# Where the transposes of x stand between two sublayers, and how y is squared and scaled

## The chip, the cores and the metric

One NeuronCore of a Trainium2 chip runs the whole kernel in one launch. The metric is device time in microseconds of that launch, the median of several executions. Engines are named as the profile names them: PE (TensorE), DVE (VectorE), ACT (ScalarE), POOL (GpSimd), SP (SyncE, which here only starts DMAs).

## The reference

Four decoder layers over a sequence of 256 tokens of width 1024, in float32. Each layer is a half-step SwiGLU FFN, a token mixer, and a second FFN. The mixers are a short gated convolution, a dilated windowed attention, an mLSTM, and the convolution again.

```python
def rmsnorm(x, g):
    y = x * rsqrt(mean(x * x, axis=-1) + 1e-6)
    return y * g

def swiglu(x, wg, wu, wd):
    return (silu(x @ wg) * (x @ wu)) @ wd       # 1024 -> 2816 -> 1024

for i in range(4):
    x = x + 0.5 * rmsnorm(swiglu(rmsnorm(x, g[0]), ...), g[1])
    x = x + rmsnorm(mixer_i(rmsnorm(x, g[2])), g[3])
    x = x + 0.5 * rmsnorm(swiglu(rmsnorm(x, g[4]), ...), g[5])
```

So between two of the twelve sublayers there is always the same seam, called a joint here: norm of y over all 1024 columns, update of x, norm of x over all 1024 columns.

## The kernel before, in words

**Tiling.** The 256 tokens are two tiles of 128 (tile 0 and tile 1), one token to a partition. Weights come in pieces of 128x2048 floats (1 MB), 352 of them, in a fixed order; SP loads them into three raw buffers. For accuracy each product is made of three: ACT rounds a piece to `w_high` (`high`, line 1039), DVE subtracts to get `w_low` (`low`, line 1421), and the other operand is split in the same way, so that `products` (lines 487 to 489) issues high x high, high x low and low x high. Split pieces stand in a ring of six. A raw buffer is free for the next load once `low` has read it, a ring slot once TensorE has used the piece (`piece_used`).

**Order of the work.** Every engine has its own program, a list written out by hand that it works off in order; a wait on a semaphore holds all that stands behind it in that engine's list. There is no planner.

**A joint.** The products of a sublayer end with y in four PSUM banks: tile 0 in two halves of 512 columns, tile 1 in two. `y_ready` tells of tile 0 as a whole, `piece_used` of tile 1 as a whole. For each tile ACT squares both halves with a running sum (`square_y`, line 1048), POOL adds the two sums and epsilon (`of_y`, line 1839) and raises to the power -1/2 (line 1843), DVE multiplies both halves by the gain (line 1432) and then updates x (line 1436). ACT squares x (line 1057), POOL adds epsilon (line 1830) and takes the power (line 1833), and DVE writes the normed xn (`pre_norm`, line 1443). TensorE turns xn in eight transposes into two banks (`transpose_x`, line 522), ACT copies them as the high half of xT (line 1063) and DVE subtracts the low half (line 1449). Only then can the next sublayer's products (`arriving`, lines 500, 503 and 506) start, which take half of the columns at a time as they arrive.

**Which transposes stand where.** Tile 0's stand at the head of each sublayer, behind all products of the one ahead. Tile 1's stand in an FFN inside its second block; in a mixer they stand at the head of tile 1's first three units (`first_three`). In the FFN's last part TensorE takes tile 0 with the last three chunks, then tile 1 with the same three; within a chunk first half 0, then half 1.

**Beside it.** At a joint ACT also makes `high(w0 + 3)` (after a mixer `high(w0 + 2)` too), where w0 is the first piece of the next sublayer, and DVE the `low` of the same. In `joint_part` of DVE, `low(w0 + 3)` stands between the update of tile 1 and its `pre_norm`; in that of ACT, `high(w0 + 3)` stands right behind the square of x of tile 0. In the attention, the 256 tokens are also wanted sorted by class (position modulo 4): `into_classes` copies the high half of xT on ACT in four copies (line 1228) and the low half on DVE in two (line 1630), all after tile 1's transposes; `rotate` is the rotary embedding on DVE, `copy_out` moves a unit's projection out of PSUM (line 1222), and `transpose_qk` (line 761) waits until some of the first six banks are free. Unit 6 is the first that reads the sorted x.

Of the kernel before, what the change touches and what calls it, by code (L numbers as in the profile page):

```python
# [25 lines left out]
ALU = mybir.AluOpType  # L26
ACT = mybir.ActivationFunctionType

P = 128
# [96 lines left out]
def build(nc, x_in, gains, stream, gate_w, gate_b, conv_k, ident_in, rope_in, att_mask_in, ml_mask_in,  # L126
          tri_in, out):
    with ExitStack() as ctx:
# [19 lines left out]
        mean_x = sb("mean_x", [P, TILES])  # L148
        mean_eps = sb("mean_eps", [P, 2 * TILES])
# [14 lines left out]
        def x_arrived(which):  # L164

            if KINDS[sub_now[0]] == "att":
                return xT_first[which]
            return xT_view(which)

# [58 lines left out]
        eps_added = sem("eps_added")  # L228
# [166 lines left out]

        def xT_bank(joint, t, b):
# [21 lines left out]
        def att_bank(quarter, n):  # L418
            if quarter == 0 and n < 6:
                return FIRST_BANKS[n // 3][n % 3]  # L420
            return 4 + n % 2

# [27 lines left out]
        def _(sp):  # L450
# [29 lines left out]
            sp.wait_ge(stored, 16 * TILES)  # L480
# [3 lines left out]
        def _(pe):  # L484
# [27 lines left out]
            def transpose_x(joint, t):  # L512
# [3 lines left out]
                for b in range(2):  # L516
# [6 lines left out]
                    last.then_inc(xT_in_psum, 1)  # L523

# [4 lines left out]
            def ffn(sub):  # L529
# [52 lines left out]
                def down(c, p, t, turn=0):  # L582

                    weights_ready(p + RING * turn)
                    for half in range(2):
                        for j in range(FT):
                            cols = slice(j * D + half * 512, j * D + half * 512 + 512)
                            tok, at = slice(t * P, (t + 1) * P), h_slot(FT * c + j)
                            if t == 1 and half == 1 and j == FT - 1 and c < CHUNKS - 1:

                                for part in range(2):
# [7 lines left out]
                                            c == 0 and j == 0, c == CHUNKS - 1 and j == FT - 1)  # L599
                    if t == 1:  # L600
                        last.then_inc(piece_used, 1)
                    elif c == CHUNKS - 1:
                        last.then_inc(y_ready, 1)
# [16 lines left out]
                transpose_x(sub, 0)  # L620
# [18 lines left out]
                for t in range(TILES):  # L639
                    for c in range(CHUNKS - 3, CHUNKS):  # L640
                        if t == 0:
                            pe.wait_ge(hT_split, s0 + splits_up_to(FT * c + 1))
                        down(c, w0 + down_piece(c), t)

            def project_out(sub):

                p0 = w_of(sub + 1) - OUT_PIECES
                for t in range(TILES):
                    tok = slice(t * P, (t + 1) * P)
                    for q in range(OUT_PIECES):  # L650
# [5 lines left out]
                        for k4 in range(4):  # L656
                            k, cols = 4 * (q // 2) + k4, slice(k4 * 512, (k4 + 1) * 512)
# [4 lines left out]
                    if t == 0:  # L662
                        last.then_inc(y_ready, 1)
# [11 lines left out]
            def tokens_first(slot, acc, t, xh=None, xl=None):  # L675

                xh, xl = (x_arrived(0), x_arrived(1)) if xh is None else (xh, xl)
                for k in range(KD):
                    tok, cols = slice(t * P, (t + 1) * P), slice(k * 256, (k + 1) * 256)
                    last = products(acc, xh[:, k, tok], xl[:, k, tok], w_high[:, slot, cols],  # L680
                                    w_low[:, slot, cols], k == 0, k == KD - 1)
                return last
# [43 lines left out]
            def attention(sub):  # L726
                w0 = w_of(sub)

                def unit(quarter, n):
# [4 lines left out]
                    if quarter == 0 and n == 6:  # L734

                        pe.wait_ge(x_by_class, KD // 2)
                        pe.wait_ge(x_low_by_class, 2)
# [4 lines left out]
                def transpose_qk(quarter, r):  # L742

                    pe.wait_ge(rope_done, 2 * QK * quarter + r + 1)
                    if r < 2 and quarter == 0:

                        pe.wait_ge(proj_copied, 3 + r)
                    elif r == 1 and quarter:

                        pe.wait_ge(oT_split, ot_before(sub) + 2 * quarter - 1)  # L750
                    elif r == 10:

                        pe.wait_ge(qkT_done, 2 * QK * quarter + 1)
                        if quarter:
                            pe.wait_ge(oT_split, ot_before(sub) + 2 * quarter)
# [4 lines left out]
                    for j in range(2):  # L760
                        last = nc.tensor.transpose(ps[:, QKT_BANK[r], j * P:(j + 1) * P],  # L761
# [133 lines left out]
                for q in (2, 3):  # L895
                    last = project_out_of(0, q, (7,))
                last.then_inc(y_ready, 1)
                for q in range(OUT_PIECES):
                    project_out_of(1, q, tuple(range(4 * (q // 2), 4 * (q // 2) + 4))).then_inc(piece_used, 1)

# [127 lines left out]
        def _(act):  # L1028
# [12 lines left out]
            def square_y(joint, t):  # L1041
                if t == 0:
                    act.wait_ge(y_ready, joint)
                else:
                    act.wait_ge(piece_used, BASE[joint])

                for half in range(2):
                    nc.scalar.activation(xn[:, t, half * 512:(half + 1) * 512], ps[:, Y_BANK + 2 * t + half, :], ACT.Square,  # L1048
# [905 lines left out]
```

## Time and profile before

| | us |
|---|---|
| median of 3 runs (2075.20 to 2076.81) | 2075.58 |
| the profiled execution's own time | 2076.98 |
| its span, first to last instruction | 2075.2 |
| PE busy | 2042.1 (98%) |
| DVE busy | 1170.3 (56%) |
| ACT busy | 970.0 (47%) |
| POOL busy | 53.3 (3%) |

Busy time is the union of an engine's instructions; for PE the ends are modelled, so short stalls between two products may not show as idle. Times given as positions count from the start of the span. "[0.97 <-ACT xT_both L1063]" behind a row means that the engine was idle for 0.97 us before it and that this instruction ended the wait.

### The profile page before, as it was taken

The page shows a single profiled execution, that of the slowest core. Times are in us where ns is not written, and L with a number is a line of the kernel's source. Part 1 is how long each engine was busy: PE and PEld are TensorE (multiplying, and loading weights), DVE is VectorE, ACT ScalarE, POOL GpSimd, SP SyncE. Part 2 cuts the span into 40 slices and gives each one's busy share as a digit, 9 for nine tenths or more (in the row PEclk, how much of TensorE's full clock was granted, in tenths as well). Part 3 has the DMA queues.
Part 4 walks back from the last instruction along what each step waited for, and adds up shares of the span by engine and source line. Part 5 has one row for each costly group of instructions (what it writes and reads, how often), then busy time and mean ns, then how long its engine had stood idle before and what let it go on. Part 6 is the DMA issues. An engine that isn't in the chain of part 4 may idle for free.

```text
span 2075.2 us, 36087 instructions
## 1 busy us (share of the span) xinstructions
PE 2042.1 (98%) x14956; PEld 1899.5 (92%) x14956; DVE 1170.3 (56%) x1328; ACT 970.0 (47%) x1184; POOL 53.3 (3%) x100
## 2 busy tenths in 40 slices
PE   7999999999999999999999999999999999999998
PEld 6999989998999899988998999898999899998997
DVE  6555765556555656556555645565545655676453
ACT  5444444444444656655444534544434444444442
POOL 0000000000000000001000000000000000000000
PEclk9999999999999999999999999999999999999999
DMA  8544646455554543435554654544554655555541
GB/s 315 201 185 161 231 154 244 182 184 203 201 186 166 180 160 143 163 122 203 199 186 170 225 204 181 194 162 152 202 203 174 223 183 184 192 192 193 203 182 62
DMA packets 55983, 386.41 MB, mean 186 GB/s; under 512 B 6592, under 2 KB 6976, under 8 KB 10816
## 3 DMA queue, kind: packets, MB, share of 16 engines
q1 hardware_dynamic: 52416, 372.66, 48.9%
q10 hardware_dynamic: 3456, 12.13, 1.7%
q8 instruction: 88, 1.44, 0.3%
q14 instruction: 23, 0.19, 0.0%
HBM read 383.71 MB, written 1.05 MB: 185 GB/s over the span
## 4 chain that ended last, share of the span: by engine, by line
PE 96%; ACT 2%; DVE 1%; issue 1%; DMA 0%; POOL 0%; ACTq 0%; POOLq 0%; SPq 0%; DVEq 0%
PE ps L487 29%; PE ps L489 29%; PE ps L488 29%; PE ps L500 2%; PE ps L503 2%; PE ps L506 2%; PE ps L522 1%; ACT w_high L1039 1%; PE ps L807 1%; PE ps L761 0%; ACT xT_both L1063 0%; PE ps L783 0%; PE ps L817 0%; PE ps L577 0%; ACT xn L1048 0%
## 5 line engine op out<-in xcount | busy, mean ns | idle before, releaser
L1421 DVE TENSOR_TENSOR w_low<-raw,w_high 128x2048 fp32r<-128x2048 f32 x352 | 804.4, 2290 | 316.2 <-ACT w_high L1039 315.8
L487 PE MATMUL ps<-xT_both,w_high 128*128 128x256 f32 x2656 | 737.1, 278 | 0.0
L488 PE MATMUL ps<-xT_both,w_high 128*128 128x256 f32 x2656 | 735.6, 277 | 0.0
L489 PE MATMUL ps<-xT_both,w_low 128*128 128x256 f32 x2656 | 735.4, 277 | 0.0
L1039 ACT ACTIVATE w_high<-raw 128x2048 fp32r<-128x2048 f32 x352 | 670.5, 1911 | 41.7 <-DMA raw<-stream 25.3
L488 PEld LDWEIGHTS ps<-xT_both,w_high 128*128 128x128 f32 x2656 | 499.9, 188 | 0.0
L487 PEld LDWEIGHTS ps<-xT_both,w_high 128*128 128x128 f32 x2656 | 499.4, 188 | 0.1
L489 PEld LDWEIGHTS ps<-xT_both,w_low 128*128 128x128 f32 x2656 | 498.6, 188 | 0.0
L1073 ACT ACTIVATE region<-ps 128x256 f32<-128x256 f32 x176 | 67.6, 384 | 659.4 <-PE ps L489 642.2
L487 PE MATMUL ps<-w_high,oT_hi 128*128 128x512 f32 (+1 forms) x944 | 348.6, 369 | 1.5 <-DVE oT_lo L1662 1.5
L488 PE MATMUL ps<-w_low,oT_hi 128*128 128x512 f32 (+1 forms) x944 | 347.5, 368 | 0.0
L489 PE MATMUL ps<-w_high,oT_lo 128*128 128x512 f32 (+1 forms) x944 | 347.4, 368 | 0.0
L1457 DVE TENSOR_TENSOR region<-region,ps 128x256 f32<-128x256 f32 x176 | 74.0, 420 | 343.5 <-ACT region L1073 343.3
L487 PE MATMUL ps<-w_high,xT_both 128*128 128x256 f32 (+1 forms) x832 | 254.2, 305 | 3.6 <-DVE xT_both L1630 1.9
L489 PE MATMUL ps<-w_high,xT_both 128*128 128x256 f32 (+1 forms) x832 | 246.8, 297 | 0.0
L488 PE MATMUL ps<-w_low,xT_both 128*128 128x256 f32 (+1 forms) x832 | 246.3, 296 | 0.0
L487 PEld LDWEIGHTS ps<-w_high,oT_hi 128*128 128x128 f32 x944 | 177.8, 188 | 31.3 <-issue 1.9
L489 PEld LDWEIGHTS ps<-w_high,oT_lo 128*128 128x128 f32 x944 | 177.7, 188 | 29.9
L488 PEld LDWEIGHTS ps<-w_low,oT_hi 128*128 128x128 f32 x944 | 177.8, 188 | 29.0
L487 PEld LDWEIGHTS ps<-w_high,xT_both 128*128 128x128 f32 x832 | 157.3, 189 | 11.2 <-issue 4.4
L489 PEld LDWEIGHTS ps<-w_high,xT_both 128*128 128x128 f32 x832 | 157.3, 189 | 5.5
L488 PEld LDWEIGHTS ps<-w_low,xT_both 128*128 128x128 f32 x832 | 157.5, 189 | 4.8
(163 smaller groups left out, 1141.7 us busy)
## 6 DMA issues: line engine op xcount, KB each, us to landing
raw<-stream SPq DMA_DIRECT2D x352, 1024.0 KB, 4.8
gain<-gains ACTq DMA_DIRECT2D x23, 512.0 KB, 4.7
x<-x_in SPq DMA_DIRECT2D x2, 512.0 KB, 6.1
out<-x SPq DMA_DIRECT2D x2, 512.0 KB, 2.7
gain<-gains SPq DMA_DIRECT2D x1, 512.0 KB, 5.3
att_mask<-att_mask_in SPq DMA_DIRECT2D x1, 384.0 KB, 5.3
region<-rope_in SPq DMA_DIRECT2D x1, 256.0 KB, 4.9
ml_mask<-ml_mask_in SPq DMA_DIRECT2D x1, 128.0 KB, 5.1
```

The costliest lines, as they stand in the source:

```text
L487: nc.tensor.matmul(acc, lh, rh, start=start, stop=False)
L488: nc.tensor.matmul(acc, lh, rl, start=False, stop=False)
L489: return nc.tensor.matmul(acc, ll, rh, start=False, stop=stop)
L500: nc.tensor.matmul(acc, x_arrived(0)[:, k, tok], w_high[:, slot, cols], start=k == 0, stop=False)
L503: nc.tensor.matmul(acc, x_arrived(1)[:, k, tok], w_high[:, slot, cols], start=False, stop=False)
L506: last = nc.tensor.matmul(acc, x_arrived(0)[:, k, tok], w_low[:, slot, cols], start=False, stop=k == KD - 1)
L522: last = nc.tensor.transpose(ps[:, xT_bank(joint, t, b), k * P:(k + 1) * P], xn[:, t, f:f + P], ident[:, :])
L807: last = nc.tensor.transpose(ps[:, bank, n * P:(n + 1) * P], probs[:, 2 * pair + e, t, col * P:(col + 1) * P], ident[:, :])
L1039: nc.scalar.activation(w_high[:, p % RING, :], raw[:, p % RAW, :], ACT.Copy).then_inc(piece_high, 1)
L1073: nc.scalar.activation(silu[:, i % 2, :], ps[:, GU_BANK + i % 2, 0:SEQ], ACT.Silu).then_inc(silu_done, 1)
L1421: nc.vector.tensor_tensor(w_low[:, p % RING, :], raw[:, p % RAW, :], w_high[:, p % RING, :], ALU.subtract).then_inc(piece_split, 1)
L1457: nc.vector.tensor_tensor(h[:, i % 2, :], silu[:, i % 2, :], ps[:, GU_BANK + i % 2, SEQ:2 * SEQ], ALU.mult).then_inc(h_ready, 1)
```

## The change

TensorE: the transposes of tile 0's xn for the next sublayer are issued ahead of the last six products of the sublayer before (in an FFN, ahead of the last chunk's second half of tile 1; in a mixer, ahead of the last two k of the last output piece). In a mixer tile 1's transposes go inside tile 0's third unit, behind k = 3. In an FFN's last part TensorE now takes half 0 of a tile for all three chunks and then half 1, and each half of y is announced by itself. ACT squares y by halves, DVE multiplies by the gain by halves; for tile 1 the copy of tile 0's xT stands between the two halves. The additions of epsilon go from POOL to DVE; POOL keeps the power. `high` and `low` of piece w0 + 3 move behind other work. In the attention the sorting copies go by tile instead of by columns (2 on each engine), tile 0's stands ahead of tile 1's xT, the copies out of units 0 and 1 and their rotations too, and the first quarter's q and k transposes use banks 2 and 3. At the very end x of tile 1 is updated and written in two halves, the second from ACT's DMA queue.

```diff
@@ sync
-                sp.dma_start(out[t * P:(t + 1) * P, :], x[:, t, :]).then_inc(stored, 16)
+                cols = slice(0, 512 if t else D)
+                sp.dma_start(out[t * P:(t + 1) * P, cols], x[:, t, cols]).then_inc(stored, 16)
@@ tensor
+            def transpose_next(sub):
+                if sub + 1 < SUBLAYERS:
+                    transpose_x(sub + 1, 0)
...
-                            if t == 1 and half == 1 and j == FT - 1 and c < CHUNKS - 1:
+                            if t == 1 and half == 1 and j == FT - 1:
...
-                transpose_x(sub, 0)
+                if sub == 0:
+                    transpose_x(sub, 0)
...
                 for t in range(TILES):
-                    for c in range(CHUNKS - 3, CHUNKS):
-                        if t == 0:
-                            pe.wait_ge(hT_split, s0 + splits_up_to(FT * c + 1))
-                        down(c, w0 + down_piece(c), t)
+                    for half in range(2):
+                        for c in range(CHUNKS - 3, CHUNKS):
+                            p = w0 + down_piece(c)
+                            if t == 0 and half == 0:
+                                pe.wait_ge(hT_split, s0 + splits_up_to(FT * c + 1))
+                                weights_ready(p)
+                            if t == 1 and half == 1 and c == CHUNKS - 1:
+                                transpose_next(sub)
+                            for j in range(FT):
+                                cols = slice(j * D + half * 512, j * D + half * 512 + 512)
+                                tok, at = slice(t * P, (t + 1) * P), h_slot(FT * c + j)
+                                last = products(ps[:, Y_BANK + 2 * t + half, :], oT_hi[:, at, tok], oT_lo[:, at, tok],
+                                                w_high[:, p % RING, cols], w_low[:, p % RING, cols], False,
+                                                c == CHUNKS - 1 and j == FT - 1)
+                            if t == 1 and half == 1:
+                                last.then_inc(piece_used, 1)
+                            elif c == CHUNKS - 1:
+                                last.then_inc(y_ready, 1)
... project_out (and the same at the end of attention)
                         for k4 in range(4):
+                            if t == 1 and q == OUT_PIECES - 1 and k4 == 2:
+                                transpose_next(sub)
... first_three
-                if first == 0:
-                    transpose_x(sub, t)
-                        done = tokens_first(p % RING, acc, t)
+                        done = tokens_first(p % RING, acc, t, meanwhile=(lambda: transpose_x(sub, 1))
+                                            if t == 0 and i == 2 else None)
... attention
-                    if r < 2 and quarter == 0:
-                        pe.wait_ge(proj_copied, 3 + r)
+                    if quarter == 0:
+                        if r >= 2:
+                            pe.wait_ge(qkT_done, r - 1)
@@ scalar, joint_part
-                    high(w0 + 3)
+                    square_y(joint, 1, 0)
+                    xT(joint, 0)
+                    square_y(joint, 1, 1)
                     if before_ffn(joint):
-                        xT(joint, 0)
-                        square_y(joint, 1)
+                        high(w0 + 3)
+                        square_x(joint, 1)
                     else:
-                        square_y(joint, 1)
-                        xT(joint, 0)
-                    square_x(joint, 1)
+                        square_x(joint, 1)
+                        if KINDS[joint] == "att":
+                            att_copy_out(joint, 0, 0)
+                            into_classes(joint, 0)
+                            att_copy_out(joint, 0, 1)
+                        high(w0 + 3)
@@ vector
+            def gain_y(joint, t, half):
+                n, cols = TILES * (joint - 1) + t, slice(half * 512, (half + 1) * 512)
+                dve.wait_ge(y_mean, 2 * n + half + 1)
+                if half == 0:
+                    nc.vector.tensor_scalar(mean_first[:, t:t + 1], mean_y[:, t, 0:1], EPS / Y_SCALE[KINDS[joint - 1]] ** 2, None,
+                                            ALU.add).then_inc(y_eps, 1)
+                else:
+                    dve.wait_ge(y_eps, n + 1)
+                    nc.vector.tensor_tensor(mean_eps[:, t:t + 1], mean_y[:, t, 1:2], mean_first[:, t:t + 1],
+                                            ALU.add).then_inc(y_sum, 1)
+                dve.wait_ge(gain_landed, 16 * min(1 + 2 * joint, 2 * SUBLAYERS))
+                nc.vector.tensor_tensor(xn[:, t, cols], ps[:, Y_BANK + 2 * t + half, :], gain[:, 0, cols],
+                                        ALU.mult).then_inc(y_gained, 1)
...
             def pre_norm(joint, t):
+                dve.wait_ge(x_mean, TILES * joint + t + 1)
+                nc.vector.tensor_scalar(mean_eps[:, TILES + t:TILES + t + 1], mean_x[:, t:t + 1], EPS, None, ALU.add).then_inc(x_sum, 1)
                 dve.wait_ge(x_rstd, TILES * joint + t + 1)
... joint_part
                 if joint:
+                    gain_y(joint, 0, 0)
+                    gain_y(joint, 0, 1)
                     update_x(joint, 0)
...
-                if joint:
+                if joint:
+                    gain_y(joint, 1, 0)
+                    if joint < SUBLAYERS:
                         xT(joint, 0)
+                    gain_y(joint, 1, 1)
                     update_x(joint, 1)
...
-                else:
+                elif before_ffn(joint):
                     low(w0 + 3)
                     pre_norm(joint, 1)
+                else:
+                    pre_norm(joint, 1)
+                    if KINDS[joint] == "att":
+                        dve.wait_ge(loaded, CONSTS)
+                        rotate(joint, 0, 0)
+                        into_classes(joint, 0)
+                        rotate(joint, 0, 1)
+                    else:
+                        low(w0 + 3)
                 if before_ffn(joint):
                     times_up(joint, 0)
                 xT(joint, 1)
+                if KINDS[joint] == "att":
+                    low(w0 + 3)
@@ gpsimd
-                nc.gpsimd.tensor_scalar(mean_eps[:, n:n + 1], mean, EPS, None, ALU.add).then_inc(eps_added, 1)
+                        pool.wait_ge(x_sum, TILES * joint + t + 1)
```

## Rows read from the trace of the kernel before

**Rows 1.** List of TensorE's waits: line, tile, releaser, us in total, times, longest.
```profile
PE ps L500 <- ACT xT_both L1063: 5.4, 13, 1.0
PE ps L761 <- ACT region L1222: 3.0, 1, 3.0
PE ps L487 <- DVE xT_both L1630: 1.9, 1, 1.9
...
PE ps L979 <- ACT region L1338: 0.8, 1, 0.8
```

**Rows 2.** Timeline of TensorE, FFN to mixer: start, duration, operation, count, idle before.
```profile
198.06 1.03 PE L522 MATMUL ps<-ident,xn 128*128 128x128 f32 x8
200.06 0.74 PE L500 MATMUL ps<-w_high,xT_both 128*128 128x256 f32 x4 [0.97 <-ACT xT_both L1063]
200.79 0.74 PE L503 MATMUL ps<-w_high,xT_both 128*128 128x256 f32 x4
201.36 0.63 PE L506 MATMUL ps<-w_low,xT_both 128*128 128x256 f32 x4
201.83 0.63 PE L500 MATMUL ps<-w_high,xT_both 128*128 128x256 f32 x4
...
208.90 1.03 PE L522 MATMUL ps<-ident,xn 128*128 128x128 f32 x8
210.19 0.74 PE L500 MATMUL ps<-w_high,xT_both 128*128 128x256 f32 x4 [0.25 <-ACT xT_both L1063]
```

**Rows 3.** Chain that ended last: transposes inside an FFN block (start, us, what).
```profile
1432.90 0.87 PE ps L522 x8
```

**Rows 4.** Timelines of VectorE and TensorE, mLSTM to FFN.
```profile
1419.50 1.29 DVE L1443 SCALAR_TENSOR_TENSOR xn<-x,rstd_x,gain 128x1024 f32<-128x1024 f32 x1 [0.77 <-POOL rstd_x L1833]
...
1422.17 0.39 PE L489 MATMUL ps<-w_high,oT_lo 128*128 128x512 f32 x1
1422.40 1.03 PE L522 MATMUL ps<-ident,xn 128*128 128x128 f32 x8
1423.69 1.21 PE L500 MATMUL ps<-w_high,xT_both 128*128 128x512 f32 x4 [0.25 <-ACT xT_both L1063]
1424.73 0.62 PE L503 MATMUL ps<-w_high,xT_both 128*128 128x512 f32 x2
```

**Rows 5.** Windows in attention: us, busy by engine (instructions), granted clock, DMA.
```profile
688.00:690.00 2.00, 2.00 (x11) 2.00 (x11) 1.97 (x1) 0.00 (x0) 0.00 (x0) 0.50 0.90 373
690.00:692.00 2.00, 2.00 (x15) 2.00 (x14) 0.00 (x0) 0.11 (x1) 0.00 (x0) 0.74 0.36 61
```

**Rows 6.** Groups by line over the whole span: busy, mean ns, idle before.
```profile
L1039 ACT ACTIVATE w_high<-raw 128x2048 fp32r<-128x2048 f32 x352 | 670.5, 1911 | 41.7 <-DMA raw<-stream 25.3 <-PE ps L489 14.9 <-issue 1.2
...
L1833 POOL TENSOR_TENSOR rstd_x<-mean_eps,minus_half 128x1 f32<-128x1 f32 x24 | 13.6, 568 | 2.0
...
L1228 ACT ACTIVATE xT_both<-oT_hi 128x512 fp32r<-128x512 f32 x4 | 4.6, 1145 | 0.0
...
L1646 DVE TENSOR_SCALAR region<-region 128x2 f32<-128x2 f32 x16 | 2.7, 170 | 0.6
```

**Rows 7.** Timelines of ScalarE, VectorE and GpSimd around the first FFN's end.
```profile
189.97 0.60 ACT L1048 ACTIVATE xn<-ps 128x512 f32<-128x512 f32 x1 [3.27 <-PE ps L489]
...
195.85 1.28 DVE L1443 SCALAR_TENSOR_TENSOR xn<-x,rstd_x,gain 128x1024 f32<-128x1024 f32 x1 [2.18 <-POOL rstd_x L1833]
...
205.12 1.01 POOL L1830 TENSOR_SCALAR mean_eps<-mean_x 128x1 f32<-128x1 f32 x1 [4.55 <-ACT xn L1057]
```

**Rows 8.** Timelines of TensorE and VectorE at the kernel's end.
```profile
2067.97 0.39 PE L489 MATMUL ps<-w_high,oT_lo 128*128 128x512 f32 x1
...
2070.81 1.28 DVE L1436 SCALAR_TENSOR_TENSOR x<-xn,rstd_y,x 128x1024 f32<-128x1024 f32 x1 [0.34 <-POOL rstd_y L1843]
```

**Rows 9.** Timelines of VectorE and TensorE at the kernel's start.
```profile
17.43 1.28 DVE L1443 SCALAR_TENSOR_TENSOR xn<-x,rstd_x,gain 128x1024 f32<-128x1024 f32 x1
...
20.97 0.50 PE L487 MATMUL ps<-w_high,xT_both 128*128 128x512 f32 x1 [1.73 <-DVE w_low L1421]
```

More of the change, by code:

```diff
@@ L394, in before_ffn, with y_before @@
             return joint < SUBLAYERS and KINDS[joint] == "ffn"
+        def y_before(joint):
+            return sum(3 if kind == "ffn" else 2 for kind in KINDS[:joint - 1])
         def xT_bank(joint, t, b):
@@ L1086, in h_high, with att_copy_out, into_classes @@
                 nc.scalar.activation(oT_hi[:, h_slot(i), :], h[:, i % 2, :], ACT.Copy).then_inc(hT_high_done, 1)
+            def att_copy_out(sub, quarter, n):
+                i, t = att_unit(quarter, n)
+                if t == 0:
+                    act.wait_ge(proj_ready, att_piece(quarter, i) + 1)
+                else:
+                    act.wait_ge(piece_used, w_of(sub) + att_piece(quarter, i) + 1)
+                at = ps[:, att_bank(quarter, n), 0:256]
+                if i > QK:
+                    for half in range(2):
+                        row = (half if i == QK + 1 else 1 - half) * CW
+                        last = nc.scalar.activation(v_rest[row:row + CW, 2 * t + half, :],
+                                                    at[half * CW:(half + 1) * CW, :], ACT.Copy)
+                    last.then_inc(proj_copied, 1)
+                    return
+                to = qk[(i - 1) % 3][:, t, :] if i else v_first[quarter % 2][:, t, :]
+                nc.scalar.activation(to, at, ACT.Copy).then_inc(proj_copied, 1)
+            def into_classes(sub, t):
+                act.wait_ge(xT_high_done, 4 * sub + 2 * t + 2)
+                nc.scalar.activation(by_class(xT_high())[:, :, :, t * CT:(t + 1) * CT],
+                                     xT_first[0][:, :, t * P:(t + 1) * P].rearrange("p k (j r) -> p k r j", r=CLASSES),
+                                     ACT.Copy).then_inc(x_by_class, 1)
             def joint_part(joint):
@@ L1424, in update_x @@
             def update_x(joint, t):
                 n = TILES * (joint - 1) + t
-                dve.wait_ge(gain_landed, 16 * min(1 + 2 * joint, 2 * SUBLAYERS))
-                for half in range(2):
-                    cols = slice(half * 512, (half + 1) * 512)
-                    dve.wait_ge(y_mean, 2 * n + half + 1)
-                    nc.vector.tensor_tensor(xn[:, t, cols], ps[:, Y_BANK + 2 * t + half, :], gain[:, 0, cols],
-                                            ALU.mult).then_inc(y_gained, 1)
@@ L1434, in update_x @@
                 dve.wait_ge(y_gained, 2 * n + 2)
                 dve.wait_ge(y_rstd, n + 1)
-                nc.vector.scalar_tensor_tensor(out=x[:, t, :], in0=xn[:, t, :], scalar=rstd_y[:, t:t + 1], in1=x[:, t, :],
-                                               op0=ALU.mult, op1=ALU.add).then_inc(x_updated, 1)
+                for half in range(2 if joint == SUBLAYERS and t else 1):
+                    cols = slice(512 * half, 512 * (half + 1)) if joint == SUBLAYERS and t else slice(0, D)
+                    nc.vector.scalar_tensor_tensor(out=x[:, t, cols], in0=xn[:, t, cols], scalar=rstd_y[:, t:t + 1],
+                                                   in1=x[:, t, cols], op0=ALU.mult, op1=ALU.add).then_inc(x_updated, 1)
```

175 lines of the change are left out of this document (77 added, 98 removed).

## The prediction

> **What bounds the kernel now.** I read the page's busy shares, then the list of what TensorE waited for, then the timeline of each seam between sublayers ("joint"). TensorE is busy nearly all the span, so time can only come from its idle stretches, from products that run slowly, and from the two ends. The list of waits [rows 1] puts these idle stretches in few places: 13 waits for the copy of the transposed x (xT, line 1063), one before a transpose of q and k in attention, one for the reordered x (line 1630), one in the mLSTM sublayer. The timeline of a joint [rows 2] shows more than the list, because ends of products are modelled. I therefore measure from start to start. Eight transposes take 0.87 us [rows 3].
>
> *FFN to mixer* (198, 660, 1311 and 1790 us; four joints). Transposes start at 198.06, so the next product could start at 198.93; it starts at 200.06, a gap of 1.13. Four products then take 0.73, 0.57 and only then 0.47 us: 0.36 more. The ACT engine squares y of tile 1 before it copies tile 0's transposes, and DVE's low half of xT is late after that. The same stands at tile 1's transposes: 208.90 + 0.87 to 210.19 is a gap of 0.42, and the slow products come again (0.36). One such joint loses 1.13 + 0.36 + 0.42 + 0.36 = 2.27 us.
>
> *To an FFN* (293, 477, 944, 1128, 1423, 1607 and 1885 us; seven joints). Transposes at 1422.40 end at 1423.27, the next product starts at 1423.69: 0.42. Four 512-column products take 1.04 against 4 x 0.23 = 0.92: 0.12. One loses 0.53 [rows 4]; tile 1's transposes already stand inside a block here.
>
> *Attention only* [rows 1, 5]. The wait before the first q and k transpose is 3.0 us in the list and the one for the reordered x 1.9. A list entry is short by what the modelled end hides (0.97 where I measured 1.13 in [rows 2]), so I take 3.2 and 2.1. Then the granted clock falls: 0.50 in 688 to 690 and 0.74 in 690 to 692, that is the lower level of 1.2 GHz for some of it. Lost there: 2 x 0.50 + 2 x 0.26 = 1.5 us. It came after two long waits close together; the gaps of 1.13 alone brought no such fall. Sum 3.2 + 2.1 + 1.5 = 6.8 us. The chain behind it is ACT's: it makes xT of tile 1, a w_high and four reordering copies of 1.15 us each [rows 6] before TensorE gets what it waits for.
>
> **The change part by part.** The sum is against the profiled execution's own 2076.98 us (span 2075.2), which is 1.4 above the median of 2075.58.
>
> *Tile 0's transposes, moved ahead of the last six products.* TensorE's work is the same, in another order. The cover is six products of 0.23 us, 1.37 us: the first transposes are seen by ACT some 0.7 us after they start, so both halves of xT (0.60 each, overlapping) are there when the last product ends. It needs xn of tile 0 earlier by 1.37, at 196.69 instead of 198.06. Before, y's squaring started at 189.97 and xn was written at 195.85 + 1.28 = 197.13 [rows 7]. The new y path takes away one square (0.60) and one of two gain products (0.68) from the chain, since y's first half is done 4 us earlier, and changes POOL's addition for a DVE one. I work out: mean 190.7, DVE's small sum 0.17 (nearest row: a 128x2 one of 170 ns [rows 6]), POOL's power 0.57 [rows 6], update 191.6 to 192.9, square 194.1, sum 194.3, power 195.0, xn 196.3. So the wait is gone with 0.4 us to spare. After a mixer, DVE makes w_low of piece w0+2 between the update and the norm, and this piece can't come sooner (ACT waits for a free slot). xn comes at 1419.50 + 1.28 = 1420.78 as before; the transposes want it at 1422.40 - 1.37 = 1421.03 [rows 4]. Cover 0.25 us, thin. If it is gone, each of these joints loses what is missing.
>
> *Tile 1's transposes inside the third unit of tile 0 (mixers).* They want xn of tile 1 60 products of 0.1175 = 7.05 us after the first arriving product, at 206.0 in this joint. The last product now ends 0.87 later than before, which moves the y chain: mean 199.85, update ends 202.0, square 203.2, xn 205.5. w_low of piece w0+3 was ahead of this norm and now is behind it; TensorE needs that piece only 10 us on, so I cost it at nothing. Cover of the transposes: 12 products, 1.41 us, enough for the two copies.
>
> So both gaps of the four joints go, 4 x 2.27 = 9.1, and 7 x 0.53 = 3.7 at the joints to an FFN. Bounds: where the thin covers fail, 6 and 2; all of it at most.
>
> *Attention.* ACT's copies of units 0 and 1 and the reordering of tile 0 now stand ahead of xT of tile 1, and the q and k transposes no longer wait for a bank. A reordering copy has 1024 elements instead of 512; ACT has two instead of four. I take 2.1 us (two of 1.15 less one fixed part). In ACT's queue from the square of tile 1 (4.2 us after the first arriving product): copy 0.3, reorder 2.1, copy 0.3, w_high 1.85, xT 1.1, two w_high 3.7, copy 0.3, reorder 2.1, two small copies 0.65, w_high 1.85, copy 0.3, gives 4.2 + 14.5 = 18.7, with hops 19.2. TensorE's own work to unit 6 is 144 products x 0.1175 + 0.87 + 3 x 0.22 = 18.5. xT of tile 1 is some 0.3 late, unit 6 some 0.5 late. Of 6.8 us I leave 0.8 as waits, and expect no fall of the clock: gain 6.0. Bounds: 3 (one long wait and the fall stay) and 6.8.
>
> *mLSTM.* TensorE waits 0.8 at the gate rows for ACT, which waits for a piece's DMA [rows 1]. That chain starts from xT of tile 1, which gains a little more than TensorE does; I take 0.4 (0 to 0.8).
>
> *Last products in another order.* Two chunks of each FFN no longer split a 512-column product in two. Two of 256 columns take 2 x 0.1175 [rows 2], one of 512 takes 0.23 [rows 4]: 48 x 0.01 = 0.5 (0 to 0.6).
>
> *End of the kernel.* From the last product's start to the update's end it is 2070.81 + 1.28 - 2067.97 = 4.12 [rows 8]. One square (0.60 in [rows 7]) goes, and 0.2 is my estimate for the shorter addition and its hop; the update comes in two halves and the last write is of half the bytes from ACT's queue. 0.8 for the chain, 0.3 for the write: 1.1 (0.6 to 1.6).
>
> *Start of the kernel: a loss.* The epsilon for x of tile 1 was added on POOL while DVE was busy; xn was written at 17.43 right behind a w_low and the product at 20.97 waits for what DVE does next [rows 9]. Now the addition stands in DVE's queue behind that w_low, and POOL's power (0.57) and two hops come after it: 0.17 + 0.57 + 0.1 = 0.8 later. Tile 0 wins some 0.15. Net -0.6 (-0.9 to +0.2).
>
> A POOL addition of 128x1 elements took 1.01 us at 205.12 while DVE was busy with a w_low; the power, a longer operation, takes 0.57 [rows 6, 7]. The Trainium skill (SBUF — State Buffer, section "SBUF: two separate sides") says that POOL and a DVE operation with two SBUF inputs lock one port pair against each other for a whole instruction. The trace agrees. By that rule alone the addition, taken off POOL, would give back most of that 1.01 us in each chain of tile 1. The queue's order says no: the DVE addition stands behind the same w_low before an FFN, and before a mixer that w_low has been moved. I take nothing for it.
>
> Sum: 9.1 + 3.7 + 6.0 + 0.4 + 0.5 + 1.1 - 0.6 = 20.2. Own time after 2056.8; median 2055.4.
>
> **The rivals.**
> *A, the waits move into the last products.* xn of tile 0 comes 0.3 to 0.8 us too late (small DVE operations and hops cost more than I took; covers are 0.4 and 0.25). 11 joints x 0.5 = 5.5 less gain: about 2061. Against it: each duration of the chain has a row.
> *B, attention stays bound by ACT and DVE.* The strided copy of 1024 elements costs more, or a w_high in between waits for its DMA; a long wait and the half clock stay: 3 to 4 less gain, 2059. For it: my margin there is already negative.
> *C, slower than before.* TensorE's queue is in order, so a late xn now holds six products and all behind them. If xn came later than TensorE by more than 20.2 / 11 = 1.84 us beyond what I have, the sum turns. With 2.5 us a joint, and the clock at half after it (1.5 a time as in attention), 11 x 4.0 = 44 against 20: about 2079 to 2100. Against it: xn was written 0.9 us before the old transposes.
> *D, no change.* The gap after the transposes is TensorE's own (weights against identity) and not ACT's copy. Then 9.1 and 3.7 mostly stay, and attention and the end give 7: 2068; if attention stays too, 2074. Against it: inside an FFN block eight transposes take 0.87 us in all in the chain that ended last, with no stall behind them [rows 3].
>
> **How the numbers follow.** Forecast 0.62, A 0.17, B 0.12, C 0.03, D 0.03, more gain than I see 0.03. The likeliest gives 2055.4; the range reaches from 2052.8 (all upper bounds) to 2061.0 (A). About 0.2% (4.2 us) is what a measurement can tell from no change: faster 0.94, same 0.03, slower 0.03.
>
> **What would show it.** Right: no gap over 0.3 us at transposes of a joint; products at 0.47 per four right after them; the wait before the first q and k transpose gone and the clock at full through attention; the power of tile 1 at the start behind w_low and the first product behind it near 21.6 instead of 20.97; from the last product to the last update 3.3 us. Wrong: TensorE waits for xn (line 1443's operation) in its list of waits, or the clock falls in a joint.

## The result: slower, 2098.4 us

The changed kernel takes 2098.38 us (median of 4 runs, 2097.22 to 2098.88) against 2075.53 for the kernel before in the same comparison: a ratio of 1.0108 [1.0091, 1.0126], 23 us slower. The prediction said 2055.4, with a range up to 2061.0. The profiled execution has a span of 2097.1 us.

The list of what TensorE waited for (line, tile, releaser, us in total, times, longest), of the changed kernel, answers to [rows 1]:
```profile
PE ps L538 <- DVE xn L1504: 8.0, 1, 8.0
PE ps L503 <- DVE w_low L1470: 2.5, 1, 2.5
PE ps L516 <- ACT w_high L1078: 1.7, 1, 1.7
PE ps L503 <- DVE oT_lo L1737: 1.5, 1, 1.5
PE ps L503 <- ACT xn L1144: 1.2, 1, 1.2
PE ps L1009 <- DVE region L1862: 0.5, 1, 0.5
```
The 13 waits for the copy of xT (5.4 us) and the one before the q and k transposes (3.0) are gone. Of the one for the reordered x (1.9) there is left a wait of 1.2 at the same place in attention, ahead of unit 6 (the line with L1144); the prediction left 0.8 in attention. The first three lines are the start of the kernel. The list adds up to 15.4 us, that of the kernel before to 26.0, and yet the kernel is slower.

The timelines of TensorE at the first joint from an FFN to a mixer, changed kernel, answering to [rows 2]: tile 0's transposes inside the last products, then tile 1's inside a unit.
```profile
202.74 1.04 PE L538 MATMUL ps<-ident,xn 128*128 128x128 f32 x8
203.53 0.48 PE L503 MATMUL ps<-w_high,oT_hi 128*128 128x512 f32 x1
...
205.00 0.63 PE L516 MATMUL ps<-w_high,xT_both 128*128 128x256 f32 x4
205.47 0.63 PE L519 MATMUL ps<-w_high,xT_both 128*128 128x256 f32 x4
...
212.00 1.03 PE L538 MATMUL ps<-ident,xn 128*128 128x128 f32 x8
212.79 0.37 PE L503 MATMUL ps<-w_high,xT_both 128*128 128x256 f32 x1
```
The first product of the mixer starts when its turn comes (205.00), and the groups of four take 0.47 at once instead of 0.74 and 0.57. Tile 1's eight transposes take 0.79 and nothing waits behind them.

So the loss is in no wait. The page of the profile shows it in the largest groups: line, engine, operation, count, busy us, mean ns of one. The products with xT moving and weights stationary (6912 of 7968 stand in FFN blocks; three lines of 2656, one shown of before and two of the changed kernel) took 278 and 277 ns before and take 282 and 281 now:
```profile
L487 PE MATMUL ps<-xT_both,w_high 128*128 128x256 f32 x2656 | 737.1, 278 | 0.0
```
```profile
L503 PE MATMUL ps<-xT_both,w_high 128*128 128x256 f32 x2656 | 747.7, 282 | 0.0
...
L505 PE MATMUL ps<-xT_both,w_low 128*128 128x256 f32 x2656 | 746.0, 281 | 0.0
```
These durations overlap, so I read the distance from start to start. Two whole FFN blocks (96 products of 256 columns, xT moving, weights stationary) with nothing between them: the first product and the 512-column one behind the last, before:
```profile
61.50 0.29 PE L487 MATMUL ps<-xT_both,w_high 128*128 128x256 f32 x1
...
72.40 0.39 PE L487 MATMUL ps<-w_high,oT_hi 128*128 128x512 f32 x1
```
and in the changed kernel:
```profile
64.01 0.28 PE L503 MATMUL ps<-xT_both,w_high 128*128 128x256 f32 x1
...
75.37 0.40 PE L503 MATMUL ps<-w_high,oT_hi 128*128 128x512 f32 x1
```
72.40 - 61.50 = 10.90 us against 75.37 - 64.01 = 11.36. One product takes 0.1135 before and 0.1183 after, at the granted clock 1.00 in both (the window of the changed kernel: us, busy and count by engine, clock, DMA):
```profile
66.00:74.00 8.00, 8.00 (x70) 8.00 (x69) 2.31 (x2) 2.49 (x3) 0.00 (x0) 1.00 0.52 214
```
An FFN has 864 such products, the worth of nine pairs, so 8 FFNs give 72 x 0.46 = 33 us: more than the 23 us lost, since what the other edits gain stands against it.

### The profile page after: what moved, and what is told of

Its sections match the earlier page's. It is cut to its first block, busy times and chain, and to the rows that moved or that the text cites. A ratio compares the mean times of both kernels' runs of the same rounds, so it can differ in the third digit from the quotient of the medians.

```text
span 2097.1 us, 36015 instructions
## 1 busy us (share of the span) xinstructions
PE 2076.0 (99%) x14908; PEld 1934.0 (92%) x14908; DVE 1177.6 (56%) x1401; ACT 972.4 (46%) x1182; POOL 26.5 (1%) x52
## 4 chain that ended last, share of the span: by engine, by line
PE 97%; ACT 1%; DVE 1%; issue 1%; DMA 0%; POOL 0%; DVEq 0%; POOLq 0%; SPq 0%
PE ps L503 30%; PE ps L504 29%; PE ps L505 29%; PE ps L519 2%; PE ps L522 2%; PE ps L516 2%; PE ps L538 1%; PE ps L844 0%; PE ps L798 0%; PE ps L820 0%; PE ps L854 0%; PE ps L598 0%; ACT w_high L1078 0%; PE ps L814 0%; DMA raw<-stream 0%
## 5 line engine op out<-in xcount | busy, mean ns | idle before, releaser
L503 PE MATMUL ps<-xT_both,w_high 128*128 128x256 f32 x2656 | 747.7, 282 | 0.0
L504 PE MATMUL ps<-xT_both,w_high 128*128 128x256 f32 x2656 | 746.3, 281 | 0.0
L505 PE MATMUL ps<-xT_both,w_low 128*128 128x256 f32 x2656 | 746.0, 281 | 0.0
```

The lines of the kernel that those rows point to most:

```text
L503: nc.tensor.matmul(acc, lh, rh, start=start, stop=False)
L504: nc.tensor.matmul(acc, lh, rl, start=False, stop=False)
L505: return nc.tensor.matmul(acc, ll, rh, start=False, stop=stop)
```

## The experiments

### What moved the products

The full diff has a hunk that the excerpt ahead of the prediction doesn't show: it allocates `mean_first`, two floats per partition, ahead of `xT_both`. Tensors are laid out in the order in which they are allocated. This one takes 32 bytes of each partition, and xT begins at byte 165216 instead of 165184. Nothing else about the products inside an FFN block changed. I tested that hunk by itself, in both kernels.

**e1_mean_last**: the changed kernel, with the small tensor behind all others that matter.
```
         mean_x = sb("mean_x", [P, TILES])
-        mean_first = sb("mean_first", [P, TILES])
...
         gate_bias = sb("gate_bias", [P, 2 * NH])
+        mean_first = sb("mean_first", [P, TILES])
```


> The changed kernel, only that the new 8-byte tensor mean_first is allocated behind all others, so that xT_both starts at byte 165184 of a partition again (a multiple of 64) and not at 165216. Theory A (address: the new tensor pushed xT and all behind it by 32 bytes, and products with 256 moving columns of xT take 0.118 instead of 0.113 us): the FFN blocks' pitch is back at 0.113 and the time is near 2056. Theory R (order: the moved transposes or the new order of instructions slow the products): pitch stays 0.118 and the time near 2098.

Measured: 2059.68 us (2056.23 to 2063.87), ratio to before 0.9918 [0.9901, 0.9934]. The same pair of blocks, in this kernel:
```profile
62.69 0.29 PE L503 MATMUL ps<-xT_both,w_high 128*128 128x256 f32 x1
...
73.58 0.39 PE L503 MATMUL ps<-w_high,oT_hi 128*128 128x512 f32 x1
```
10.89 us, the value of before. With this hunk moved, the change gains 15 us instead of losing 23.

**e2_before_pad**: the kernel before, with an unused tensor of 8 bytes at the same place, and nothing of the change.
```
         mean_x = sb("mean_x", [P, TILES])
+        mean_first = sb("mean_first", [P, TILES])
```


> The kernel before with an unused 8-byte tensor at the place where the change puts mean_first, nothing else. Theory A: the time rises by what the changed kernel lost in pitch, some 8 x 864 products x 0.005 = 35 us for the FFNs and a few for the mixers, to 2110 to 2120. Theory R: 2075.5 as before.

Measured: 2115.94 us (2115.52 to 2117.5), ratio 1.0196 [1.0179, 1.0213]. Against 2075.00 for the kernel before in the same comparison, a tensor that no instruction touches costs 41 us. The pair of blocks takes 73.16 - 61.80 = 11.36:
```profile
61.80 0.28 PE L488 MATMUL ps<-xT_both,w_high 128*128 128x256 f32 x1
...
73.16 0.40 PE L488 MATMUL ps<-w_high,oT_hi 128*128 128x512 f32 x1
```

**e4_only_xT_aligned**: is it xT's own alignment? 165184 is a multiple of 64, 165216 is not. Here the changed kernel puts xT at 165248, a multiple of 64 again: all ahead of it stays, and its tensor grows by 64 bytes.
```
-X_SHIFT = {"ffn": 0, "conv": 0, "att": 32, "ml": 32}
+X_SHIFT = {"ffn": 8, "conv": 8, "att": 40, "ml": 40}
```


> The changed kernel with mean_first where it is; xT is taken 8 floats (32 bytes) further on inside its tensor, so it alone starts at a multiple of 64 bytes again, while ident, region and all behind them stay at 32 beyond one. Theory A in its narrow form (xT's own address decides): near 2056, pitch 0.113. If ident's or region's address were what matters: near 2098. Theory R: near 2098.

Measured: 2109.45 us (2109.17 to 2115.52), ratio 1.0172 [1.0155, 1.0189]. Worse than 32 bytes off: 74.48 - 62.96 = 11.52 for the pair. A multiple of 64 is not the rule.
```profile
62.96 0.28 PE L503 MATMUL ps<-xT_both,w_high 128*128 128x256 f32 x1
...
74.48 0.40 PE L503 MATMUL ps<-w_high,oT_hi 128*128 128x512 f32 x1
```

**e3_sweep** and **e6_sweep_wide**: e1, with another offset of xT in each of the 8 FFNs, so that one execution gives eight points. The shifts are in floats, by sublayer, the first line of e3 and the second of e6.
```
+SHIFTS = (0, 32, 4, 8, 32, 16, 24, 32, 32, 48, 8, 40)
...
+SHIFTS = (64, 0, 128, 256, 32, 320, 1, 32, 4, 56, 0, 60)
...
-            at = X_SHIFT[KINDS[sub_now[0]]] + which * KD * SEQ
+            at = SHIFTS[sub_now[0]] + which * KD * SEQ
```


> The kernel of e1 with another start of xT in each sublayer: for the eight FFNs in order 0, 16, 32, 64, 96, 128, 192 and 160 bytes beyond a multiple of 64, for the two convolutions 128 and 32, attention and mLSTM 128 as before. Theory A: the pitch of an FFN's blocks depends on the offset: 0.113 at 0, 0.118 at 32, and the others tell the period (64 if 64, 128 and 192 give 0.113). Theory R: the same pitch in all eight.

> The kernel of e1 with xT of the eight FFNs 256, 512, 1024, 1280, 4, 16, 224 and 240 bytes beyond its place before. A period of 256 bytes (theory A2a): 0.113 at 256, 512, 1024 and 1280, more at the others; at 4 bytes more than 0.113, at 16 the 0.119 that the first sweep had there being 16 bytes too. A period of 1024 (A2b): 0.113 at 1024 alone. None (A2c): 0.118 to 0.120 at all.

Each was run once (2093.91 and 2085.91 us); only the distances inside that execution are used. Measured, the mean distance from start to start of an FFN's 912 products of 256 columns (864 with xT moving; the other 48 have no xT and keep 118.7 to 118.8 ns throughout), by the offset from 165184:

| offset, bytes | 0 | 4 | 16 | 32 | 64 | 96 | 128 | 160 | 192 | 224 | 240 | 256, 512, 1024, 1280 |
|---|---|---|---|---|---|---|---|---|---|---|---|---|
| ns | 113.9 | 121.6 | 119.3 | 118.5 | 120.0 | 118.0 | 118.0 | 120.0 | 118.8 | 117.5 | 119.4 | 113.9 to 114.0 |

Of the offsets tried, only multiples of 256 bytes are fast. The offsets 16, 32 and 64 were each measured in two kernels (e3 with e6, with the changed kernel and with e4), to the same result. The pair of blocks of the second sweep at +4 bytes (11.68 us):
```profile
1205.13 0.29 PE L503 MATMUL ps<-xT_both,w_high 128*128 128x256 f32 x1
...
1216.81 0.40 PE L503 MATMUL ps<-w_high,oT_hi 128*128 128x512 f32 x1
```

**e5_all_shifted**: is it xT's address modulo 256, or its distance from the weights? Here the small tensor stands ahead of the weights too. xT is at 165216, the slow address, but w_high and w_low have moved with it.
```
+        mean_first = sb("mean_first", [P, TILES])
         raw = sb("raw", [P, RAW, PIECE])
...
         mean_x = sb("mean_x", [P, TILES])
-        mean_first = sb("mean_first", [P, TILES])
```


> The changed kernel with mean_first allocated ahead of all other tensors of the kernel: w_high, w_low and xT all start 32 bytes further on, their distance from each other is that of the kernel before. Theory A1 (the distance between the weights and xT decides): pitch of the FFN blocks 0.113, time near 2060. Theory A2 (xT's own address decides): pitch 0.118, time near 2098.

Measured: 2058.42 us (2055.59 to 2060.31), ratio 0.9916 [0.9899, 0.9932]; the pair of blocks 74.92 - 64.02 = 10.90:
```profile
64.02 0.29 PE L503 MATMUL ps<-xT_both,w_high 128*128 128x256 f32 x1
...
74.92 0.39 PE L503 MATMUL ps<-w_high,oT_hi 128*128 128x512 f32 x1
```
The address is that of the slow kernel, the distance that of the fast one, and the products are fast. So xT's own address is not what decides; its distance from what stands ahead of it is: xT less w_high is 139456 = 544 x 256 + 192 bytes and xT less w_low 90304 = 352 x 256 + 192 in before, e1 and e5, and 32 more in the changed kernel and e2.

All tensors ahead of xT moved together in e5, also the raw buffers that DMA fills and oT, the operand that takes xT's place in the other products. Two readings of the traces leave the weights as the tensor that counts. The first is a sum by kind of product, of the distances from its start to the next start on TensorE, in us. e5 (span 2056.3) and the changed kernel (2097.1) have the same order of work, and nearly the same waits:

| product | number | e5 | changed kernel |
|---|---|---|---|
| xT moving, 256 columns | 7968 | 911.4 | 944.6 |
| xT stationary, 256 columns of weights moving | 2256 | 267.4 | 273.4 |
| xT stationary, 512 | 768 | 184.2 | 186.8 |
| oT stationary, 512 | 2303 | 526.3 | 525.8 |
| oT stationary, 256 | 528 | 63.1 | 63.1 |

The products with xT are 41.8 us longer, those with oT, whose distance from the weights no edit changed, 0.5 shorter. The second is a stretch without DMA and without ScalarE, VectorE and GpSimd, in windows of the changed kernel and of e5:
```profile
2071.50:2075.00 3.50, 3.50 (x32) 3.50 (x31) 0.00 (x0) 0.00 (x0) 0.00 (x0) 1.00 0.00 0
```
```profile
2031.30:2034.30 3.00, 3.00 (x29) 3.00 (x28) 0.00 (x0) 0.00 (x0) 0.00 (x0) 1.00 0.00 0
```
The products with xT moving take 118.3 ns from start to start in the first and 113.4 in the second, as in the busy stretches. So no access of another engine or of a DMA is needed for it: what counts is the distance between the two operands of the product.

The Trainium skill (TensorE: Matmul & The Clock Gate, section "Part 2: What happens when you issue a matmul") gives TensorE two independent SBUF read ports, so that the load of the next weights doesn't steal bandwidth from the running product. It names no dependence on where the two operands lie, and these runs show one: xT 32 bytes farther from the weights makes a product with xT moving 4% longer, 4 bytes farther 7%. Whether the load of the weights has a part in it, no run separates.

### Why e1 gained 15.3 and not 20.2

The profiled execution of e1 has a span of 2062.0, 7 us over the 2055.0 that the prediction amounts to. TensorE's waits in it:
```profile
PE ps L1018 <- ACT region L1387: 2.6, 1, 2.6
PE ps L503 <- ACT xn L1144: 2.5, 1, 2.5
```
The second is in attention. ACT's timeline there:
```profile
672.08 2.12 ACT L1149 ACTIVATE xT_both<-oT_hi 128x1024 fp32r<-128x1024 f32 x1
...
677.45 1.91 ACT L1078 ACTIVATE w_high<-raw 128x2048 fp32r<-128x2048 f32 x1 [2.71 <-DMA raw<-stream]
```
The reordering copy takes 2.12 as predicted (2.1), and the queue is on time. But the w_high behind it waits 2.71 for its load. The load needs the slot of raw that `low(w0 + 3)` frees, and that one stands behind tile 1's whole xT in VectorE's queue: the first w_low of the group at 668.67. SyncE issues the load when it is done, at 671.13, and it takes 6.3 us. VectorE's and SyncE's timelines:
```profile
668.67 6.69 DVE L1470 TENSOR_TENSOR w_low<-raw,w_high 128x2048 fp32r<-128x2048 f32 x3
```
```profile
671.13 4.74 SPq L487 DMA_DIRECT2D raw<-stream  x3
```
Then the clock falls, in the windows:
```profile
680.00:682.00 2.00, 2.00 (x11) 2.00 (x11) 1.97 (x4) 2.00 (x3) 0.00 (x0) 0.50 0.73 307
682.00:684.00 2.00, 2.00 (x14) 2.00 (x14) 1.97 (x7) 0.25 (x1) 0.00 (x0) 0.67 0.52 127
```
Level 0.50 (1.2 GHz) held for 3.4 us, which costs 1.7. With the gap of 2.78 from start to start, attention loses 4.5 us where the prediction left 0.8. The wait in mLSTM is of the same kind: ACT waits 3.16 and 2.03 us for loads, TensorE 2.6, and the clock falls for another 3.4 us (1.7): 4.3 where I left 0.4. Excess 3.7 + 3.9 = 7.6, about the 7 missing in this execution. It is the longest of e1's four (2063.87). The profile of e5, with the same order of work, has a wait of 1.4 in attention and none at the gates of mLSTM, and the clock stays at 1.00 in both; the changed kernel has 1.2 and none. In all three the wait in attention stands behind a load that ACT waits for (2.71, 1.54 and 1.29 us).

**e7_att_order**: e1, and in attention the weights' work stands ahead of tile 1's: `high(w0 + 3)` before the square of x, `low(w0 + 3)` right behind tile 1's norm and ahead of the rotation and reordering.
```
+                    elif KINDS[joint] == "att":
+                        high(w0 + 3)
+                        square_x(joint, 1)
+                        att_copy_out(joint, 0, 0)
+                        into_classes(joint, 0)
+                        att_copy_out(joint, 0, 1)
... vector
                     pre_norm(joint, 1)
...
+                    low(w0 + 3)
```


> The kernel of e1 with piece w0 + 3 of the attention split earlier: high ahead of the square of x of tile 1, low right behind its norm, so that the DMA into the freed raw buffer starts some 4 us sooner. Theory W (the waits left in attention, 2.7 us and the fall of the clock behind it, hang on that DMA): the wait before unit 6 goes under 0.5 us, no clock of 0.5 in attention, 3 to 4.5 us less than e1, near 2056. Rival (ACT's copies themselves are late): within 1 us of e1.

Measured: 2056.65 us (2055.53 to 2057.15), ratio 0.9908 [0.9891, 0.9924]: 3.0 us less than e1, 1.8 less than e5. TensorE has no wait in attention, and ACT waits 0.59 for the load. So the wait, there in all three profiles of the old order, is gone as expected; the gain in time is hardly more than e1's and e5's runs differ among themselves.

**e8_all_orders**: e7, and the same in mLSTM (`high(w0 + 3)` ahead of tile 1's square, `high(w0 + 4)` ahead of its xT), and at the start of the kernel tile 1's epsilon ahead of the w_low.
```
+                    elif KINDS[joint] == "ml":
+                        high(w0 + 3)
+                        square_x(joint, 1)
+                        high(w0 + 4)
...
+                    add_eps(joint, 1)
                     low(1)
```


> The kernel of e7, and the same for the mLSTM (high of w0 + 3 and w0 + 4 ahead, so that the chain over the DMA into ACT's copy of the gates starts sooner), and at the very start the addition of epsilon for tile 1 ahead of a w_low. Theory W: the wait at the gates under 1 us and no clock of 0.5 there, 3 to 4 us; at the start 0.7 us; near 2051. Rival: the gates' copy waits for the gain DMAs' issue on ACT's queue, then the wait stays above 2 us and the gain is under 1.5.

Measured: 2054.58 us (2054.14 to 2055.56), ratio 0.9899 [0.9883, 0.9916]: 20.8 us faster than before, 43.8 faster than the change as it was made. Waits of TensorE, all of them:
```profile
PE ps L538 <- DVE xn L1514: 8.2, 1, 8.2
PE ps L516 <- ACT w_high L1078: 1.7, 1, 1.7
PE ps L503 <- DVE oT_lo L1745: 1.5, 1, 1.5
PE ps L1009 <- DVE region L1870: 0.5, 1, 0.5
PE ps L503 <- DVE w_low L1476: 0.4, 1, 0.4
```
TensorE has no wait of a load's making left in attention or mLSTM, and the clock stays at 1.00 from 17.9 us to the end of the products.

Of the 3.7 to 4.7 us that were expected over e7, 2.1 came, and they are not mLSTM's: e7's profile has no wait at the gates and no fall of the clock there either. They are at the start. Counted from TensorE's first transposes, the product behind the start's w_low comes at 13.5 us in e7 and at 12.7 in e8; and in e7 TensorE waits 2.0 for it and the clock falls to 0.50 for 3.4 us behind it (1.7 lost), in e8 it waits 0.4 and the clock stays. The changed kernel and e5 have the same wait (2.5 and 2.6) and the same fall, e1 has 1.4 and no fall. Windows of the changed kernel:
```profile
22.00:24.00 2.00, 2.00 (x6) 1.59 (x5) 1.95 (x2) 0.20 (x1) 0.00 (x0) 0.50 0.70 205
24.00:26.00 2.00, 2.00 (x8) 1.60 (x7) 0.00 (x0) 0.00 (x0) 0.00 (x0) 0.73 0.97 383
```
From e1 to e8 the medians differ by 5.1 us, from e5 to e8 by 3.8. I credit the new order in attention and at the start together with about that. Whether the order in mLSTM gains anything is not shown: its wait is in one profile of four of the old order (e1, not the changed kernel, e5 or e7). The issue of a gain's DMA held ACT's queue there for 1.60 us in e1, 1.22 in e5, 1.42 in e7 and 0.45 in e8, and what part it has in the late loads no run separates.

## Why the prediction was wrong

*The step that failed* is "TensorE's work is the same, in another order", and with it the assumption, made without a word, that each product keeps its pace: the sum has no term for it. The instructions are the same, but their operands lie 32 bytes farther apart. With the distance restored the changed kernel gives 2059.68 and 2058.42, inside the range; without it, 2098.38, which is 38.7 and 40.0 more. The products with xT account for it: 41.8 us between the profiles of e5 and of the changed kernel, whose spans differ by 40.8. About 31 of it is the FFNs' (8 x 864 products of 118.4 instead of 113.9 ns). No rival had this mechanism. A and D are refuted: no wait moved into the last products, and no gap is left behind the transposes. Rival C put the loss in late xn, and was wrong: its range held the time by chance.

*Joints to a mixer and to an FFN* (9.1 and 3.7): right. At all eleven joints the eight transposes of either tile take 0.79 us from the first to the next product's start, in the changed kernel as in e1, and the mixer's first groups of four take 0.47. (The one product behind eight transposes takes 0.31 instead of 0.23, as it did inside an FFN before.) The gaps before were a little larger than I had: eight transposes take 0.79 from start to start there too, at tile 1 of a joint to an FFN, where I read 0.87 off the chain [rows 3]. The thin covers held, at the joints behind a mixer too (xn is written 0.29 to 0.30 us ahead, I had 0.25): xn of tile 0 was needed by the transposes at 202.74 and written at 201.06 + 1.29 = 202.35. VectorE's timeline at the joint, changed kernel, answering to [rows 7]:
```profile
196.85 0.16 DVE L1482 TENSOR_TENSOR mean_eps<-mean_y,mean_first 128x1 f32<-128x1 f32 x1 [0.60 <-ACT xn L1087]
...
197.75 1.28 DVE L1495 SCALAR_TENSOR_TENSOR x<-xn,rstd_y,x 128x1024 f32<-128x1024 f32 x1
...
201.06 1.29 DVE L1504 SCALAR_TENSOR_TENSOR xn<-x,rstd_x,gain 128x1024 f32<-128x1024 f32 x1 [0.66 <-POOL rstd_x L1911]
```
From the start of y's last square (ACT, 196.13) to the end of xn it takes 6.2 us; I had 6.3 (189.97 to 196.3), and the 0.4 us to spare is 0.39.

*Attention* (6.0): mechanism half right, size wrong. The copies and their prices came as worked out, the wait for a bank went, but the term "w_high 1.85" in my queue assumed that its load was there. It is rival B's condition, which I gave 0.12. e7 shows that the wait hangs on the place of w_low and w_high in the two queues. *mLSTM* (0.4): not there where the loads are late, 4.3 lost instead in e1; no run shows that the order is the cause.

*Last products in another order* (0.5): right. The 96 products of 256 columns that are gone took 120 ns each, the 48 of 512 that came for them 227 (both medians): 0.6 us.

*POOL's addition* (nothing taken): at the joint of [rows 7] it ends at 206.13, 0.08 us behind the w_low that ends at 203.76 + 2.29 = 206.05. So do all 16 of the 24 additions that ran beside a w_low; the other 8 took 0.22. From the end of tile 1's square of x to the start of its xn there were 1.77 us and are 0.84, and TensorE waited for neither.

*End* (1.1): from the last product to the end of the update 3.46 in e1 and 3.45 in the changed kernel, against 4.12 before and 3.3 forecast. From the last product to the end of the span it is 5.9 against 7.2, so 1.3 gained: a little less in the chain than forecast, more in the write. Changed kernel, answering to [rows 8]:
```profile
2091.12 0.39 PE L505 MATMUL ps<-w_high,oT_lo 128*128 128x512 f32 x1
```
```profile
2093.16 1.41 DVE L1495 SCALAR_TENSOR_TENSOR x<-xn,rstd_y,x 128x512 f32<-128x512 f32 x2
```

*Start* (-0.6): right in mechanism, but not the whole cost. e1's epsilon, power and xn are at 17.38, 17.60 and 18.19, xn 0.76 late (I had 0.8). In e8, with the epsilon ahead of w_low, xn starts at 17.31:
```profile
17.38 0.15 DVE L1500 TENSOR_SCALAR mean_eps<-mean_x 128x1 f32<-128x1 f32 x1
18.19 1.29 DVE L1504 SCALAR_TENSOR_TENSOR xn<-x,rstd_x,gain 128x1024 f32<-128x1024 f32 x1 [0.67 <-POOL rstd_x L1911]
```
```profile
17.31 1.28 DVE L1514 SCALAR_TENSOR_TENSOR xn<-x,rstd_x,gain 128x1024 f32<-128x1024 f32 x1
```
Counted from TensorE's first transposes, the product behind it starts at 12.65 in before, at 13.47 in e1, 13.48 in the changed kernel, and 12.69 in e8, which gives the 0.8 back. The fall of the clock behind it, 1.7 us in the changed kernel, e5 and e7, I had not seen coming.

*The sum*: 20.2 was forecast from the order of the work. e1 gives 15.3 and e5 17.0. e8 gives 20.8, but with three edits that the prediction didn't have, one of which mends the loss that it had counted at the start. So the terms of the joints, the last products and the end hold, those of attention, mLSTM and the start were too good for the change as it was made, by 3 to 5 us in all, and the 39 to 40 us of the operands' distance had no term.

**What stays open.** At the good distance the products of 256 columns run at 0.1135 in most of an FFN, but at about 0.118 in its first blocks and in most of the mixers, in before as in e1. Here is a stretch of FFN 0 of before, three products in 0.36 us from 44.33 (0.12 each), then a whole block of 48 in 5.46 (0.1138).
```profile
44.33 0.28 PE L489 MATMUL ps<-xT_both,w_low 128*128 128x256 f32 x1
...
44.69 0.28 PE L489 MATMUL ps<-xT_both,w_low 128*128 128x256 f32 x1
...
50.55 0.29 PE L487 MATMUL ps<-xT_both,w_high 128*128 128x256 f32 x1
...
56.01 0.39 PE L487 MATMUL ps<-w_high,oT_hi 128*128 128x512 f32 x1
```
I saw it change from one to the other in the middle of a stage, at places where transposes stand, and ran nothing on it. Nor does any run say why a distance modulo 256 matters, or whether a distance other than those of the table, or of other operands, would be faster still. For the 512-column products with xT stationary one of the table is: their median is 229 ns at the distance of before, 234 at 32 bytes more and 227 at 64 more (e4).

## What to carry to other kernels

When a diff adds, removes or resizes a tensor, list where every operand of the hot instruction lies before and after, and treat a moved address as an edit of its own: here 8 unused bytes cost 41 us of 2075. When time changes and the waits don't, compare the distance from start to start of the commonest instruction first. And where a chain's next item is made from a streamed load, its slot must come free earlier than the item is due by the longest load seen, not by the median one (here 4.8 us in the median, 6.3 at this place, 7.7 in e1's mLSTM), so a move of the operation that frees the slot is a move of the load.

## Behaviour of the hardware not expected

- A product of 128x128 weights and 256 moving columns takes from start to start 113.9 ns at a distance of xT from the weights of 192 modulo 256 bytes, and 117.5 to 121.6 at the ten others tried. The Trainium skill (TensorE: Matmul & The Clock Gate, section "Back-to-back issue gap") gives N/2.4 + 2.5 ns for an isolated product at the full clock, by which 256 columns take 109.2 (an estimate from that page), and knows no such dependence; the best measured is 4.7 ns over it.
- The shift of 32 bytes moves the median of the 512-column products with xT stationary from 229 to 234 ns and leaves that of those with oT stationary, whose distance it doesn't change, at 227.
- The granted clock fell to 0.50 for 3.4 us behind TensorE's waits of 2.5 us (attention) and 2.6 (mLSTM) in e1, and behind those of 2.5, 2.6 and 2.0 at the start of the changed kernel, e5 and e7. It stayed at 1.00 behind the 1.4 in e5's attention, the 1.7 at the start of before and the joints' gaps of 1.13 us [rows 2]. It stayed there behind the 3.0 in before's attention too and fell only behind the next one, of 1.9, so the length of the last wait doesn't tell it alone.
